# First block of a four-layer network: w_ada rows on TensorE around one half GEMM, the affine rows by ACT, w_ada sums behind each attention step, the row norm by halves

## The reference

```python
mod = silu(c) @ w_ada + b_ada                      # c: [1, 1024], w_ada: [1024, 3072]
shift, scale, gate = split(mod, 3)
h = rms_norm(x, norm_g) * (1 + scale) + shift      # x: [256, 1024]
z = h @ w_in                                       # w_in: [1024, 2976]
c_q, c_kv, k_rope, g_mla, q_b, k_b, v_b, g_moba = split(z)   # 256 128 32 512 512 512 512 512
o_mla  = mla_attention(c_q, c_kv, k_rope, ...)     # 8 heads: q = rms_norm(c_q) @ w_uq (768),
                                                   # kv = rms_norm(c_kv) @ w_ukv (1024), norms, rope
o_moba = moba_attention(q_b, k_b, v_b, ..., rel_bias)   # 8 heads of 64, here causal attention with bias
y = concat(silu(g_mla) * o_mla, silu(g_moba) * o_moba) @ w_out
x = x + gate * y
```

## Time and profile before

| | us |
|---|---|
| median of three runs | 1696.76 (1690.75 to 1697.41) |
| profiled execution, its time | 1694.23 |
| its span | 1692.4 |
| PE busy | 1600.2 (95%) |
| DVE busy | 1067.8 (63%) |
| ACT busy | 855.9 (51%) |
| mean granted clock of TensorE | 0.988 |

### The profile page before, as it was taken

One profiled execution on the slowest core, in us unless ns is written; L12 is line 12 of the kernel. 1 busy time (PEld: TensorE's weight loads), 2 busy tenths in 40 slices (PEclk: granted clock), 3 DMA queues, 4 the chain that ended last, 5 costly groups with the idle time before them and its releaser, 6 DMA issues.

```text
span 1692.4 us, 21793 instructions
## 1 busy us (share of the span) xinstructions
PE 1600.2 (95%) x7796; PEld 1318.4 (78%) x7796; DVE 1067.8 (63%) x1792; ACT 855.9 (51%) x1487; POOL 123.9 (7%) x157
## 2 busy tenths in 40 slices
PE   1679989999999999999999999999999999999998
PEld 1567778778888778878788887888878787788886
DVE  5778577666565646567666556565555567675653
ACT  0346536645444565555454445444455655464442
POOL 3011002100000200002100000000020001200000
PEclk9989989999999999999999999999999999999999
DMA  9565257435555664455565556555582454656552
GB/s 286 199 233 191 74 188 237 132 113 185 188 183 192 160 188 120 136 150 156 187 208 170 194 188 191 186 176 193 174 222 79 130 174 125 205 187 191 178 190 75
DMA packets 155336, 293.27 MB, mean 173 GB/s; under 512 B 10214, under 2 KB 23316, under 8 KB 155228
## 3 DMA queue, kind: packets, MB, share of 16 engines
q1 hardware_dynamic: 149312, 276.60, 50.7%
q0 software_dynamic: 4800, 12.29, 3.1%
q10 hardware_dynamic: 1116, 2.99, 0.5%
HBM read 290.77 MB, written 1.06 MB: 172 GB/s over the span
## 4 chain that ended last, share of the span: by engine, by line
PE 79%; DVE 8%; DMA 5%; ACT 3%; issue 2%; POOL 1%; SPq 0%; DVEq 0%; POOLq 0%; ACTq 0%
PE pb L444 75%; PE pb L448 4%; DMA raw<-in_w_in 3%; DVE wl L1312 2%; DVE acc L1309 1%; DMA raw<-in_w_ada 1%; POOL st L2074 1%; ACT wh L814 1%; DVE xt_l L1309 1%; ACT xt_h L814 1%; DVE dg L1306 0%; DVE h L1309 0%; ACT pb L814 0%; DVE xt_l L1312 0%; DVE pb L1315 0%
## 5 line engine op out<-in xcount | busy, mean ns | idle before, releaser
L814 ACT ACTIVATE wh<-raw 128x1024 fp32r<-128x1024 f32 (+1 forms) x484 | 505.9, 1051 | 454.0 <-PE pb L444 391.5
L1312 DVE TENSOR_TENSOR wl<-raw,wh 128x1024 fp32r<-128x1024 f32 (+1 forms) x484 | 581.4, 1219 | 208.7 <-ACT wh L814 204.6
L444 PE MATMUL pb<-wh,xt_h 128*128 128x512 f32 (+2 forms) x1536 | 593.0, 386 | 12.0 <-ACT wh L814 9.9
L444 PE MATMUL pb<-wl,xt_h 128*128 128x512 f32 (+2 forms) x1536 | 584.8, 381 | 11.9 <-DVE wl L1312 11.8
L444 PE MATMUL pb<-wh,xt_l 128*128 128x512 f32 (+2 forms) x1536 | 585.8, 381 | 1.9 <-DVE xt_l L1309 1.7
L444 PEld LDWEIGHTS pb<-wh,xt_h 128*128 128x128 f32 x1536 | 291.8, 190 | 68.4 <-ACT xt_h L814 10.8
L444 PEld LDWEIGHTS pb<-wl,xt_h 128*128 128x128 f32 x1536 | 292.0, 190 | 64.0 <-DVE wl L1312 13.7
L444 PEld LDWEIGHTS pb<-wh,xt_l 128*128 128x128 f32 x1536 | 291.4, 190 | 62.1 <-DVE xt_l L1309 8.5
L444 PE MATMUL pb<-wh,big_h 128*128 128x512 f32 x352 | 138.7, 394 | 0.0
L444 PE MATMUL pb<-wl,big_h 128*128 128x512 f32 x352 | 138.6, 394 | 0.0
L2074 POOL TENSOR_TENSOR st<-st,cols 128x1 f32<-128x1 f32 (+2 forms) x56 | 53.0, 952 | 1146.6 <-DVE st L1309 759.4
(11 more groups left out here) (205 smaller groups left out, 1478.0 us busy)
## 6 DMA issues: line engine op xcount, KB each, us to landing
raw<-in_ffn_w_gu SPq DMA_DIRECT2D x176, 512.0 KB, 4.5
raw<-in_w_in SPq DMA_DIRECT2D x148, 512.0 KB, 4.3
raw<-in_ffn_w_down SPq DMA_DIRECT2D x88, 512.0 KB, 3.7
raw<-in_w_ada SPq DMA_DIRECT2D x48, 512.0 KB, 5.5
raw<-in_w_out SPq DMA_DIRECT2D x32, 512.0 KB, 4.3
raw<-in_w_branch SPq DMA_DIRECT2D x24, 512.0 KB, 3.6
raw<-in_w_in SPq DMA_DIRECT2D x8, 416.0 KB, 4.0
G<-in_na_rpb POOLq DMA_DIRECT2D x32, 96.0 KB, 8.5
```

The costliest lines, as they stand in the source:

```text
L444: return e.matmul(o, a, b, start=start, stop=stop)
L814: return e.activation(o, a, func, **kw)
L1312: return e.tensor_tensor(o, a, b, op)
```

## The change

At the start tiles (0,2) and (0,3) are no longer weighed by DVE: PE multiplies silu(c), as a 128x1 operand, with each half of a chunk, in float32, into one row of bank 7 (`ada_row`); ACT copies the row out (`row_out`) and `turn_both` turns it and the tile that DVE weighs, (0,0) or (0,1), together. The first four rows of x^T are then made, and the first half of z's GEMM (`part=0`) stands ahead of the second pair of tiles. The squares and the variance are taken by halves of 512, one of the two row blocks is scaled by ACT. The affine step moves from DVE to ACT (two 128x256 with scale and bias, one 128x512 copy for `xt_h`; DVE one 128x512 subtraction). In layer 1 z and qb are each in two halves as well. x is issued ahead of the small rows, the constants later in pieces, and the ten `bc` loads move from POOL to SP, behind chunks from 36 on.

The norms of z, qb and kb become ten side steps (`norms`), the transposes of q go into the vb GEMM (`mid=turn_q`), those of c stand behind kb, those of k behind q0. Side tiles of w_ada have new places: in layer 0 (1,0) and (1,1) in lat, (0,4), (0,5) in the moba gate, (1,2) in out; (1,3) in layer 1's z, (1,4) in its lat and (1,5) in its moba gate. There are three `acc` buffers, the third being `dg`.

In DVE's `split` a w_ada chunk is no longer weighed where it stands in `plan`: it goes into the queue `weights`, and is weighed at a take once its number is at most that of the GEMM chunk k+4, less NRAW - 1.

```diff
-    first_tiles = [(0, j) for j in (0, 2, 1, 3)]
-    side_tiles = {(0, 0): [(1, 0), (1, 1), (1, 2), (0, 4), (0, 5)], (0, 1): [(1, 3)], (1, 0): [(1, 4), (1, 5)], (1, 1): []}
-    ada_tiles = first_tiles + [x for k in sorted(side_tiles) for x in side_tiles[k]]
-    ada_no = {x: i for i, x in enumerate(ada_tiles)}
+    side_tiles = {("lat", 0): [(1, 0), (1, 1)], ("gmoba", 0): [(0, 4), (0, 5)], ("out", 0): [(1, 2)],
+                  ("lat", 1): [(1, 4)], ("gmoba", 1): [(1, 5)], ("out", 1): []}
+    acc_tiles = [(0, 0), (0, 1)] + [x for x in side_tiles["lat", 0] + side_tiles["gmoba", 0]] + [
+        (1, 2), (1, 3), (1, 4), (1, 5)]
+    acc_no = {x: i for i, x in enumerate(acc_tiles)}
+    acc = acc + [dg]
...
+        def ada_row(l, j, kq):
+
+            c = ada_chunk(l, j, kq)
+            v = chunk_view(raw[c % NRAW], c)
+            if kq == 0:
+                open_bank(7, ("sum", l, j))
+            w.wait_ge(*at("csil"))
+            w.wait_ge(*at(f"raw{c % NRAW}", c))
+            for k in range(2):
+                kx = 2 * kq + k
+                last = mm(banks[7][0:1, :], stat(8, "c_silu")[:, kx:kx + 1], v[:, k, :], kx == 0, kx == 7)
+            last.then_inc(*up("row", l, j, kq))
...
+        def turn_both(l, j, j2):
+
+            b = rot("mod", l, j2)
+            w.wait_ge(*at("one"))
+            w.wait_ge(*at("sum", l, j2))
+            for f in range(4):
+                mm(b[:, 4 + f:5 + f], row_sum(l, j2)[:, f * 128:f * 128 + 128], ones_col[0:1, :], True, True)
+            w.wait_ge(*at("acc", l, j, 7))
+            for f in range(4):
+                last = mm(b[:, f:f + 1], acc[acc_no[l, j] % 3][:, f * 128:f * 128 + 128], ones_col, True, True)
+            last.then_inc(*up("turn", l, j))
...
+        win = d["w_in"][0]
+        for kq in range(4):
+            ada_chunk(0, 0, kq)
+            ada_row(0, 2, kq)
+            if kq == 1:
+                b = rot("cols")
+                w.wait_ge(*at("rows"))
+                tr(b[:, 0:126], rows[0:126, :]).then_inc(*up("rtr"))
+        turn_x(0, 0)
+        turn_both(0, 0, 2)
+        ada_chunk(0, 1, 0)
+        ada_row(0, 3, 0)
+        take_early(("z", 0), win, 0, 416, [(0, 2), (2, 2)])
+        gemm(("z", 0), XT, 0, xkey0, win, 0, 416, "eva", part=0)
+        for kq in range(1, 4):
+            ada_chunk(0, 1, kq)
+            ada_row(0, 3, kq)
+            if kq == 2:
+                turn_x(0, 4)
+        take_early(("z", 0), win, 0, 416, [(4, 2), (6, 2)])
+        turn_both(0, 1, 3)
...
+            def turn_q():
+                turn_heads(("mobaq", l), lambda j, t: qkv[:, t, j * 128:j * 128 + 128], 4, 128,
+                           lambda t: [("nrm", "qb", l, t)])
+
+            gemm(("vb", l), XT, 0, xkey, win, 1952, 512, "eva", mid=turn_q)
+            gemm(("q0", l), XC, 0, ckey, d["mla_w_uq"][l], 0, 512, "eva")
...
+        def rows_squares(l, m, ready):
             for t in range(2):
                 w.wait_ge(*at(*ready(t)))
                 old_read(XT)
-                ac_(xn[:, t, :], h[:, t, :], ACT.Square,
-                    accum_out=stat(1, "rn", l, t)).then_inc(*up("rsq", l, t))
-
-        for _ in range(7):
-            next(first)
-        rows_norm(0, lambda t: ("x",))
-        for _ in range(8):
-            next(first)
+                ac_(xn[:, t, m:m + 512], h[:, t, m:m + 512], ACT.Square,
+                    accum_out=stat(1, "rn", l, t, m)).then_inc(*up("rsq", l, t, m))
+
+        def rows_scale(l):
+            w.wait_ge(*at("rs", "rn", l, 1))
+            for m in (0, 512):
+                ac_(xn[:, 1, m:m + 512], h[:, 1, m:m + 512], scale=stat(1, "rs", "rn", l, 1)).then_inc(
+                    *up("xn1", l, m))
+
+        def turn_x(l, c0):
+
+            for c in range(c0, c0 + 4, 2):
+                b = rot()
+                v = xtmp[c // 2 % 2]
+                w.wait_ge(*at("tr", ("x", l), c))
+                w.wait_ge(*at("ac", l, c0 // 4))
+                if ("x", l, c) in lower_of:
+                    w.wait_ge(*at(*lower_of["x", l, c]))
+                for j in range(2):
+                    ac_(v[:, j * 256:j * 256 + 256], b[:, j * 256:j * 256 + 256], ACT.Identity,
+                        scale=ac[l][:, c + j:c + j + 1], bias=mod[:, l, c + j:c + j + 1]).then_inc(
+                        *up("xm", ("x", l), c + j))
+                w.wait_ge(*at("xm", ("x", l), c + 1))
+                old_read(XT)
+                ac_(xt_h[:, c:c + 2, :], v.rearrange("p (c n) -> p c n", n=256)).then_inc(*up("xh", ("x", l), c + 1))
+                yield
...
+        rows_scale(0)
+        split(stream.lead(8))
+        for a0, a1 in ((C_CAUS, C_INV), (C_ZERO, C_OH)):
+            e.dma_start(cst[:, a0:a1], d["consts"][:, a0:a1]).then_inc(*landed("cst"))
+        row_out(0, 2)
+        first = turn_x(0, 0)
+        next(first)
+        split(stream.lead(3))
+        next(first)
+        rot()
+        split(stream.lead(1))
+        split(stream.lead(6))
+        row_out(0, 3)
+        second = turn_x(0, 4)
...
+            side.add(norms(), 10)
+            side.over(10 if l else 12)
...
+
         def split(chunks):
 
             for c in chunks:
-                src, kk, n, _, i, ada_ = plan[c]
-                if ada_:
-                    weigh(c)
-                    continue
-                w.wait_ge(*at("hi", c))
-                if i >= NW:
-                    w.wait_ge(*at(*plan[split_at[i - NW]][3]))
-                w.wait_ge(*at(f"raw{c % NRAW}", c))
-                tt(wl[i % NW][:, 0:kk * n], raw[c % NRAW][:, 0:kk * n], wh[i % NW][:, 0:kk * n].bitcast(F),
-                   ALU.subtract).then_inc(*up("lo", c))
+                if plan[c][5]:
+                    weights.append(c)
+                else:
+                    lower_part(c)
+            i = min(stream.taken + AHEAD, len(split_at) - 1)
+            while weights and weights[0] <= split_at[i] - NRAW + 1:
+                weigh(weights.popleft())
...
+        weigh_next(2)
+        w.wait_ge(*at("pos"))
+        e.tensor_copy(stat(2, "pos"), posi[:, :]).then_inc(*up("posf"))
+        w.wait_ge(*at("posf"))
+        w.wait_ge(*at("inv"))
+        for t in range(2):
+            ts(ang[:, 0, t * 16:t * 16 + 16], cst[:, C_INV:C_INV + 16], stat(2, "pos")[:, t:t + 1], None,
+               ALU.mult, None).then_inc(*up("ang0", t))
+        rows_half(0)
+        rows_var(0)
+        weigh_next(2)
+        rows_scale(0)
+        reduce_angle(0)
+        b = rot()
+        w.wait_ge(*at("rtr"))
+        e.tensor_copy(cols[:, 8:126], b[:, 8:126]).then_inc(*up("cols"))
+        weigh_next(2)
+        reduce_angle(1)
+        weigh_next(2)
+        first = turn_x(0, 0)
+        next(first)
+        turn_both(0, 0, 2)
+        factors(0, 0)
+        weigh_next(2)
+        next(first)
+        split(stream.lead(1))
+        next(first)
+        z1 = stream.lead(1)
+        weigh_next(2)
+        split(z1)
+        weigh_next(4)
+        second = turn_x(0, 4)
+        next(second)
+        turn_both(0, 1, 3)
+        factors(0, 1)
+        next(second)
+        split(stream.lead(1))
+        next(second)
+        split(stream.lead(1))
+
         def rope1(v, nh, t, key):
             wv, before = turn_of_temp(("rope", *key))
...
-        for name, a0, n in bc_in:
-            e.dma_start(bc[:, a0:a0 + n], bass.AP(tensor=d[name].tensor, offset=0, ap=[[0, 128], [1, n]])).then_inc(
-                *landed("bc"))
...
+            if c >= 36 and vectors:
+                name, a0, m = vectors.popleft()
+                e.dma_start(bc[:, a0:a0 + m], bass.AP(tensor=d[name].tensor, offset=0, ap=[[0, 128], [1, m]])).then_inc(
+                    *landed("bc"))
```

More of the change, by code:

```diff
@@ L211, in early, with groups @@
         return due
-def groups(nk, n, head, tail):
+def groups(nk, n, head, tail, part=None):
     per = 1024 // n
     chunks = [(c0, min(per, nk - c0)) for c0 in range(0, nk, per)]
+    if part is not None:
+        m = len(chunks) // 2
+        return [[c] for c in (chunks[m:] if part else chunks[:m])]
     tail = min(tail, len(chunks) - head)
@@ L501, in gemm, with to_xt @@
                 for _ in taken:
+                    later.fill()
                     side.fill()
[L503 to L507 removed]
+        def to_xt(s, src, nch, ready, by="xl", c0=0):
+            for c in range(c0, nch, 2):
                 m = min(2, nch - c)
@@ L983, in act @@
         ac_(stat(8, "c_t"), cols[:, 0:8], ACT.Tanh, scale=0.5).then_inc(*up("ctanh"))
-        stream.lead(16)
-        first = ada(first_tiles)
-        for _ in range(5):
-            next(first)
-        e.dma_start(mq[0:32, 0, 0:512], d["consts"][0:32, C_OH:C_END]).then_inc(*landed("oh"))
+        load_rows(rows_in[1:])
         rot()
-        def rows_norm(l, ready):
+        def rows_squares(l, m, ready):
             for t in range(2):
@@ L1091, in act @@
             side.drain()
-            later.add((None for _ in range(4)), 4)
-            later.add(ada(side_tiles[l, 1]), 5 * len(side_tiles[l, 1]))
```

(31 more changed lines are left out.)

441 lines of the change are left out of this document (266 added, 175 removed).

## The result

The changed kernel takes 1737.87 us (median of four runs, 1734.17 to 1739.85) where the one before takes 1694.07: a ratio of 1.026, 95% interval 1.022 to 1.029. I had forecast slower, at 1708 within 1673 to 1722. The sign was right, and so was the mechanism that I had put first, but it cost far more than I gave it: 43.8 us instead of 13.4.

The account below looks back on a forecast made before the run. The first block was bound by the chain to z's first matmul, then PE's own work. Terms -32.5 + 19.8 + 23.1 + 1 + 2 = +13.4 on 1694.2 gave 1707.6, forecast 1708 us, range 1673 to 1722.

Parts of the forecast that it names:

- the mechanism that I had put first: Case A, whole kernel: late weighing eats the start's gain and more; 1708 us, own range 1696 to 1720, chance 0.5.
- the start: Start to vb's end, layer 0: x lands at 15, z ends about 55.5, vb at 90.9; gain 32.5 us, bounds 27 and 38.
- Rival D: Start brings less: x lands after 20, w_ada's 18th chunk after 46; gain 15, costs as in A, 1725 us, chance 0.1.
- the late weighing: vb's end to mla transposes: ACT waits for buffers held by DVE's late sums; +19.8 us in layer 0, +23.1 in layer 1.
- rival C: DVE and ACT get so far ahead of PE that weighing is done when ACT asks; 1663 us, chance 0.1.
- B: Rival: the waits for late weighing are there but half as long; -9 us, 1685, chance 0.2.
- its two terms: Late weighing from vb's end to the mla transposes: layer 0 +19.8 us (bounds 8 and 28), layer 1 +23.1 (7 and 27).
- Side tiles in the moba gate and w_out: one more late chunk, +1: Moba gate and w_out: side tiles there bring one more late chunk, +1 us.
- layer 1's start at 0: Layer 1's start: first half GEMM begins 1.3 us earlier, a pause of about 2 before its second half takes that back: 0.
- lie under other work: Two of layer 0's late places, at the start of the moba gate's steps and in w_out, hold up no attention steps.
- the stage of layer 0: vb's end to mla transposes: 63.6 us instead of 43.8, from waits of 26.7 and PE's own work of 36.9; +19.8.
- The clock. [...] I take +2: PE matmuls after waits run slow, but a slow PE only fills its own idle time in these rounds; +2 us.

Follow-up runs that it names:

- fillers: Changed kernel plus 8 matmuls of 128x512 that nobody reads in each of moba's attention steps, ahead of the wait for its probabilities: 1733.22 us, ratio 1.023.

## Why the prediction was right in its sign and wrong in its size

By its own terms, in us of the profiled executions, from TensorE's landmarks. "Late" is the changed kernel less the one that weighs at once, "rest" is that one less the kernel before. The forecast is put on the same landmarks: q0's first matmul stood at 127.86 before, so 4.5 of what the prediction counted in the stage lies ahead of it here.

| stretch | forecast | measured | late | rest |
|---|---|---|---|---|
| start to q0, layer 0 | -37.0 | -37.4 | 1.1 | -38.5 |
| q0 to mla transposes, layer 0 | 24.3 | 30.4 | 14.1 | 16.3 |
| moba gate, to w_out's transposes | 1 | 5.9 | 8.7 | -2.8 |
| w_out, to z of layer 1 | 0 | 9.0 | 10.4 | -1.4 |
| z to q0, layer 1 | -0.8 | 3.6 | 2.9 | 0.7 |
| q0 to mla transposes, layer 1 | 23.9 | 27.9 | 21.1 | 6.7 |
| moba gate, layer 1 | 0 | 1.2 | 2.8 | -1.6 |
| all behind it | 2 | 5.1 | -0.1 | 5.3 |
| sum | 13.4 | 45.7 | 61.0 | -15.3 |

**Right: the start.** Its chain was off by up to 4 us in its steps (x landed at 11.4 and not 15, the first half GEMM began at 28.6 and not 30.8, the second half ended at 55.1 and not 55.5), and its gain by 0.4. That it is so close is in part luck: x landed outside my bounds of 12 to 20, and the second half began 1.3 earlier than I had it (47.0 against 48.3) but took 0.9 longer, its matmuls 0.35 us apart up to 52.65 and 0.19 behind. Rival D, x landing after 20, is refuted.

**Right: the late weighing** is what made the change slower; rival C, that it is hidden, is refuted, and so is B, half the waits. It was worth 61 us, against the 43 of its two terms. Of these 61 the two stages that I had priced hold 35, less than the 43, and the stretches that I had taken for free hold most of the rest.

**Wrong: "Side tiles in the moba gate and w_out: one more late chunk, +1", and layer 1's start at 0.** I wrote that two of the places "lie under other work" and did not walk their chains. What stood behind the late sums cost 8.7 in the gate and 10.4 in w_out; layer 1's start is 2.9 longer than with weighing at once, which is within what that stretch varies by. Against the kernel before these three stretches are 18.5 longer where I had 0.2, over half of the error of 32.3. In w_out ACT waited 8.10 for a chunk, PE 4.3 for a sum itself, and layer 1's rows waited for their scale, 6.19 (the row at 241.86; 3.1 with weighing at once), since DVE had sums to catch up on ahead of it. The places were also counted too narrowly: the kernel before with late weighing loses 34 us where the order has none of them.

**Wrong in its makeup: the stage of layer 0.** I forecast 24.3 and put all of it on the late weighing. That brought 14.1; 16.3 came from what I did not price: two tiles in seven chunks (10 of it went away with one tile moved, of which the moba gate took 4.7 back), and some 6 whose cause stays open. The split is good to about 3 us, since with weighing at once this stage took 55.6 in one kernel and 52.3 in another. My count of PE's waits, 26.7, was too high, 19.9 were measured in this stage, and my 36.9 for its own work too low, 49.8. In part this is the clock that I kept out of the sum (I had even taken 2.2 us of slow matmuls out): matmuls at half speed took the place of idle time, and with fillers the own work falls to 45.4 or less at a clock of 0.87. In layer 1 it is the same: 19.8 of waits against my 23.8, and 44.6 of work against 36.6.

**Wrong: "The clock. [...] I take +2".** The reason, that a slow TensorE only fills idle time, holds in the rounds that the late chunk closes: with fillers 14.8 us more of matmuls went into a stage that got 1.0 shorter. It does not hold behind them. In the moba gate of layer 0 TensorE is the bound again, and its busy time is 37.4 us in the changed kernel and 30.6 in the one that weighs at once, where the clock is 1.00: 6.8 of the 8.7 there are slower matmuls. About 2 of the 6.8 lie at the gate's start, where the clock is still at half from the waits ahead (0.50 from 160 to 165). One wait of 2.44 us was followed by about 5 us of loss (the three pieces at 0.57, 0.50 and 0.90); that the fall comes of the wait fits the rows, but no run took this wait alone away. My own row of before gave 1.6 for a wait of 2.39, too low for this one. The Trainium skill, TensorE: Matmul & The Clock Gate, HAM oscillation, tells of waits for DMA of about 3 to 5 us that cool TensorE each time. The rows here show half clock behind a shorter wait. By the price that the Trainium skill has for it, half of 1.67 us, this wait would be an estimated 0.8.

**Open.** The stretch behind the first block is 5.1 longer in the profile, though the change adds nothing there; 2.9 of it are two waits for mqt at the mixers' starts (2.0 each, 0.6 before), and the other experiments' profiles show 1.1 to 6.2. I did not settle the rest. Nor did I settle what the slower clock costs in the first block as a whole.

## What to carry to other kernels

Before an engine's work is put off, look for who waits for the buffer that this work holds: here a sum that nobody needed yet held a ring slot, the transfer into it and a third engine's in-order queue stood behind it, and 61 us went by with no more work on any engine. Price such a place everywhere it stands in the order, also where other work seems to cover it, and let the distance in the stream, not the moment of need, set how late is allowed; one chunk of it gave back 50 us. A change of several parts can hide a gain: this one's start was worth 33 us, and with the one line undone and one tile moved it is 1.3% faster than the kernel before.

## What the runs showed of the hardware

Ten vectors broadcast to 128 partitions, 0.7 MB together, held back x (1 MB) by 5.7 us and the fourth w_ada chunk by 6.8, where at the 256 GB/s of the earlier trace rows their bytes are 2.9 us. I had not expected their cost to be twice that of their bytes. The rows of the queues fit: the 0.73 MB took 7.9% of 60 us on all 16 DMA engines, 4.7 us or 6.5 per MB, where `q1` took 37.8 us for 12.72 MB, 3.0 per MB. Whether the broadcast or POOL's queue makes the difference no run here shows.
